# Where the dense steps stand between the level products of a chunked RWKV-7 scan

## The reference, cut to what matters

```python
cols = rms_norm(x) @ w_in                 # q k v | r k v + LoRA | two gates
o_attn = banded_gqa_attention(q, k, v, sink)
def step(S, inp):                         # per head, forward and backward in time
    r_t, w_t, k_t, v_t, a_t, b_t = inp
    sa = S @ a_t
    S = S * w_t + outer(sa, b_t) + outer(v_t, k_t)
    return S, S @ r_t
merged = sigmoid(g_a) * o_attn + sigmoid(g_r) * o_rwkv
h = x + rms_norm(merged @ w_out)
h = h + rms_norm(relu(rms_norm(h) @ w_ffn_up) ** 2 @ w_ffn_down)
```

## Time and profile before

| | us |
|---|---|
| median of 3 runs | 2063.53 (2062.06 to 2068.5) |
| the profiled execution, whole | 2065.07 |
| its span | 2063.3 |
| TensorE busy in the span | 1993.1 (97%) |
| VectorE busy | 1317.3 (64%) |
| ScalarE busy | 927.3 (45%) |
| GpSimd busy | 371.0 (18%) |
| one pair, in the steady stretch | 53.33 |

### The profile page before, as it was taken

How to read it: one execution, slowest core, us unless ns; L and a number is a source line. 1 busy time by engine, 2 the same in 40 slices (tenths; PEclk the granted TensorE clock), 3 DMA queues, 4 the chain that set the end, 5 groups by cost and what they waited for, 6 DMA issues and landing times.

```text
span 2063.3 us, 39449 instructions
## 1 busy us (share of the span) xinstructions
PE 1993.1 (97%) x14555; PEld 1841.9 (89%) x14555; DVE 1317.3 (64%) x2226; ACT 927.3 (45%) x1669; POOL 371.0 (18%) x438
## 2 busy tenths in 40 slices
PE   6999999899999999999999999999999999999997
PEld 6999999899999999999999878899898989989896
DVE  3666546677777777777777864655555555555554
ACT  4555433344444454545445543543443434334343
POOL 0000000333343333344444440100000000000001
PEclk9999999899999999999999999999999999999999
DMA  7555666433223333233331326356566565656553
GB/s 209 136 142 140 182 163 170 109 89 82 77 78 87 88 88 87 77 79 87 88 88 47 123 86 226 103 187 184 187 184 188 184 182 192 183 183 183 184 182 122
DMA packets 415375, 281.28 MB, mean 136 GB/s; under 512 B 14074, under 2 KB 372700, under 8 KB 414556
## 3 DMA queue, kind: packets, MB, share of 16 engines
q1 hardware_dynamic: 414908, 277.43, 46.5%
q10 hardware_dynamic: 416, 3.15, 0.4%
HBM read 278.46 MB, written 2.10 MB: 136 GB/s over the span
## 4 chain that ended last, share of the span: by engine, by line
PE 90%; DVE 3%; issue 2%; ACT 2%; POOL 1%; DMA 0%; SPq 0%; ACTq 0%; DVEq 0%; POOLq 0%
PE bank L1512 16%; PE bank L1513 15%; PE bank L1514 15%; PE bank L1532 6%; PE bank L1531 6%; PE bank L1530 6%; PE bank L1753 2%; PE bank L1797 2%; PE bank L1815 2%; PE bank L1820 2%; PE bank L1658 1%; PE bank L1882 1%; PE bank L1660 1%; PE bank L1861 1%; PE bank L1659 1%
## 5 line engine op out<-in xcount | busy, mean ns | idle before, releaser
L1512 PE MATMUL bank<-xT,whi 128*128 128x256 f32 x2784 | 823.6, 296 | 12.1 <-DVE wlo L848 8.0
L1513 PE MATMUL bank<-xT,whi 128*128 128x256 f32 x2784 | 789.1, 283 | 0.0
L1514 PE MATMUL bank<-xT,wlo 128*128 128x256 f32 x2784 | 788.4, 283 | 0.0
L1512 PEld LDWEIGHTS bank<-xT,whi 128*128 128x128 f32 x2784 | 535.1, 192 | 15.1 <-issue 9.1
L1513 PEld LDWEIGHTS bank<-xT,whi 128*128 128x128 f32 x2784 | 535.6, 192 | 1.9
L1514 PEld LDWEIGHTS bank<-xT,wlo 128*128 128x128 f32 x2784 | 534.1, 192 | 0.0
L848 DVE TENSOR_TENSOR wlo<-raw,whi 128x1024 fp32r<-128x1024 f32 (+1 forms) x164 | 247.0, 1521 | 58.7 <-ACT whi L440 54.1
L1353 DVE TENSOR_TENSOR wlo<-raw,whi 128x1024 fp32r<-128x1024 f32 x126 | 154.4, 1225 | 200.7 <-ACT whi L810 200.7
L810 ACT ACTIVATE whi<-raw 128x1024 fp32r<-128x1024 f32 x126 | 132.8, 1054 | 216.9 <-PE bank L1532 216.9
L1531 PE MATMUL bank<-wlo,ft 128*128 128x512 f32 x512 | 202.2, 395 | 0.0
L1532 PE MATMUL bank<-whi,ft 128*128 128x512 f32 x512 | 202.2, 395 | 0.0
(11 more groups left out here) (224 smaller groups left out, 3072.4 us busy)
## 6 DMA issues: line engine op xcount, KB each, us to landing
raw<-in_w_in SPq DMA_DIRECT2D x106, 1024.0 KB, 5.9
raw<-in_w_ffn_up SPq DMA_DIRECT2D x64, 1024.0 KB, 6.4
raw<-in_w_ffn_down SPq DMA_DIRECT2D x64, 1024.0 KB, 5.0
raw<-in_w_out SPq DMA_DIRECT2D x16, 1024.0 KB, 5.5
raw<-in_w_in SPq DMA_DIRECT2D x4, 768.0 KB, 4.6
xtok<-in_x SPq DMA_DIRECT2D x2, 1024.0 KB, 5.9
upg<-in_g_up SPq DMA_DIRECT2D x16, 128.0 KB, 3.4
hres<-in_x ACTq DMA_DIRECT2D x1, 2048.0 KB, 12.3
```

Source lines behind the costliest of these rows:

```text
L1512: M(bank[:, 0:T], h, xT[:, k, 0, :], start=k == 0, stop=False)
L1513: M(bank[:, 0:T], h, xT[:, k, 1, :], start=False, stop=False)
L1514: x = M(bank[:, 0:T], l, xT[:, k, 0, :], start=False, stop=k == KT - 1)
```

## The change

Each level's steps are put together: the first portion of a level takes both numbers, the second is empty, and `filler` returns at once when it is asked for none. The sum of each level stays (4, 4, 5, 5, 5, 3), and so does the total of 26. The steps stand behind D1(l-1) (in level 1 the second transpose) and ahead of D0(l); between W1(l) and W0(l+1) no step is left, nor between W1(6) and D1(6).

```diff
         EARLY = 2
-        STEPS = ((2, 2), (2, 2), (2, 3), (3, 2), (3, 2), (1, 2))
+        STEPS = ((4, 0), (4, 0), (5, 0), (5, 0), (5, 0), (3, 0))
 ...
                 def filler(count):
 
+                    if not count:
+                        return
                     k = at[0]
                     at[0] = k + count
```

## The result

The changed kernel took 2105.84 us (median of 4 runs, 2105.71 to 2107.95), the kernel before 2063.61 us beside it. The ratio is 1.0197, 95% interval 1.0183 to 1.0211: 42.2 us slower by the medians, 38 to 44 by the interval of the ratio, where 46 were forecast.

A forecast was written before the change was run, and what follows sets the result against it. TensorE, busy 97% of the span, was taken as the bound. Per pair, 2.76 + 0.21 + 0.77 + 0.1 - 0.75 - 0.2 = 2.89 us; 16 pairs give 46 us, so 2110 us, range 2096 to 2126.

The forecast's parts named there:

- Gaps before W0(3) to W0(6): Levels 2 to 6: without second portions, TensorE waits 0.69 us before each of these products, 2.76 us a pair.
- Level 1, no net change: Filling the 0.65 us wait before D0(1) opens about 0.7 us before W0(2): 0 us net.
- The end: Before D1(6), the wait for ScalarE's copy lies 0.70 us open, plus 0.07 us restart: 0.77 us a pair.
- The wait at W1(6): The 0.34 us wait for level 5's block-1 addition goes, with three steps ahead of D0(6) instead of one.
- VectorE's other work: Neighbour sum and half cut make level 5's first addition late by 0.1 us, costing 0.1 us a pair.
- No absorption: Behind the levels TensorE had only 0.08 us idle in 32.30 us, so no delay is absorbed there.
- B: Rival: VectorE's other work delays additions in level 5; 3.5 to 4.1 us a pair, 2120 to 2129 us; 9%.
- C: Rival: waits filled, VectorE trip hidden, no new gap; a pair gains 1.09 us, 2046 us; 2%.
- E: Rival: one or two of five gaps don't open; 2.1 or 1.4 us a pair, 2086 to 2098 us; 7%.
- D: Rival: the clock falls once a pair, losing 2.9 us; 5.8 us a pair, 2156 us; 3%.

The follow-up runs named there:

- e2: The kernel before with only level 2's four steps put together in the first portion: 2074.66 us, ratio 1.0038.
- e9: The kernel before with one step left in the second portion of levels 1 to 5, level 6 unchanged: 2082.25 us, ratio 1.0080.
- e5: The changed kernel with D's two products and VectorE's two additions turned round, those for Dm first: 2094.80 us, ratio 1.0144 to the kernel before.
- e1: The kernel before with only level 1's four steps put together in the first portion: 2062.67 us, ratio 0.9986.
- e3: The kernel before with only level 6's three steps put together in the first portion: 2068.49 us, ratio 1.0017.
- e4: The kernel before with all steps of every level in the second portion, none in the first: 2125.03 us, ratio 1.0279.
- e11: As e4, but with level 1's four steps in the first portion: 2121.63 us, ratio 1.0274 to the kernel before.

## Why the prediction was right

The direction, the mechanism and the size held: 46 us forecast, 42 measured. Point by point, for a pair:

- *Gaps before W0(3) to W0(6)*: release 1.31 us behind D0 forecast, 1.31 and 1.32 measured. e2 priced one at 0.73 us (0.69 + 0.07 - 0.04 forecast), e9 showed that it shrinks with the step that fills it, e5 that W0 keeps its 0.10 us to the end of VectorE's addition when that comes earlier. The trace prints 0.53 us for each gap, where 0.69 to 0.70 lie between the end of the work that TensorE had and the next start, since the drain of the product before is counted as busy; a forecast of printed waits (0.6 to 0.7) was wrong in that, the one of start-to-start distances was right.
- *Level 1, no net change*: D0(1) to W0(2) is 1.49 us before and after, and e1 gave 0.01 us.
- *The end*: 0.77 us forecast; D1(6) is 0.86 us behind W1(6), not 0.95, so 0.61 us and the restart. The term was too large by 0.1: ScalarE's copy ended 0.80 us behind W1(6), not 0.84, and the release took 0.06 us, not 0.11. Why is not shown; that W1(6) came behind a wait before and doesn't now is not enough, since in e5 D1(2) starts 0.94 us behind a W1(2) that had not waited. The wait at W1(6) closed as forecast. e3 gave 0.33 for 0.30 together.
- *VectorE's other work*: 0.1 us forecast, 0 measured. Its neighbour sum, 811.91 to 813.13, delayed the block-1 additions of level 4: D1(4) started at 812.35, so the first of them was due 0.46 us later, at 812.81, and started at 813.06. But the cut behind them (813.72 to 814.93) was done before the block-0 addition of level 5 was due, at 815.08. The prediction had it end 4.4 us behind D0(4), and it ended 4.15 behind: the working set printed durations end to end, where the next instruction starts some 0.07 us before the printed end of the one before (the sum at 811.91, the addition ahead of it until 811.99).
- *No absorption*: 32.41 us behind the levels against 32.30.

Sum: 2.89 forecast, 2.71 measured. The two over-sized terms, 0.09 and 0.1 us, make up the difference. Of the rivals, B (VectorE in the way) is refuted by the rows above, C (faster) by the sign, E (gaps don't open) by five open gaps. D (the clock falls) didn't happen in this change: the level stages ran at full clock, but for that of the first pair, where the clock was low before the change too. Yet e4 and e11 show that it is no idle threat, though its price of 2.9 us a fall was too high: 1.0 to 1.4 us were measured. The Trainium skill, page "TensorE: Matmul & The Clock Gate", section "A second HAM failure mode: psum-queue depth-cycling", says that frequent short idle times between groups of matmuls can throw the clock back and forth. The trace of e11 agrees so far as the clock fell to 1.2 GHz in 750.60:753.90 with no printed gap over 0.54 us in the level stage ahead of it; the changed kernel, with gaps of 0.53 us each 3.84 us, stayed at full clock. Why the one and not the other is open.

## What to carry to other kernels

Where a matmul engine works off a chain that goes round two other engines, independent work must stand in each place where it would wait, and how much is read from the rows: the start of the product to the end of the last instruction it waits for, plus the release, less the products already in between. Before moving such work, look at the wait that is hidden behind the one you shorten (e5: 1.7 us expected, 0.67 got). And let the engine next in the chain do first what is waited for first: that order alone was worth 10 us here, and with the steps dealt anew 15.

## What the runs showed of the hardware

The granted clock fell to 1.2 GHz in e11 with no printed gap over 0.54 us in the level stage ahead of it; in the changed kernel, with more such gaps (95 waits of TensorE before its W and D products against 50 in e11), it stayed at 2.4 GHz from 459.02 to 1244.90. A pair with a fall took 1.0 to 1.4 us more in e4 (57.62 to 58.03 against 56.60) and 1.4 us more in e11 (57.37 against 55.93). What makes the difference was not tried.

The label "issue" stood on waits for another engine: where it was followed up, the product started 0.10 us behind the end of VectorE's addition, and in e5, where that addition came 0.42 us earlier behind D0, the product did too. Such a wait is best checked against the ends of all its possible releasers, and a gap by the distance from start to start: in e5 some 0.28 us stayed open ahead of W0 in levels 2 to 5 and were printed nowhere.
